# Depthwise convolution accumulated in two PSUM banks, four PSUM banks left for projections, and another order of projections, pooling, layer norm and modulation

## The chip, the cores and the metric

The kernel runs on one core of a Trainium2 chip. Time is the device time of one execution, in microseconds (us). The engines of the core are PE (TensorE: matrix products), DVE (VectorE), ACT (ScalarE), POOL (GpSimd) and SP (SyncE, which here only issues transfers). Matrix products write to PSUM, a memory of eight banks of 128 x 512 float32 each; DVE and ACT read and write PSUM too. Everything else lies in SBUF.

## The reference

One decoder layer over 2048 tokens of width 1024, in float32. A conditioning vector gives shift, scale and gate for both halves. Four mixers of 256 channels share one input projection:

```
def reference(x, c, w_ada, b_ada, norm1_g, ...):
    mod = (silu(c) @ w_ada + b_ada)
    sh1, sc1, g1, sh2, sc2, g2 = split(mod, 6)
    h = rms_norm(x, norm1_g) * (1.0 + sc1) + sh1
    qa, ka, va, ub, uc, ud = split(h @ w_in, IN_SPLITS)
    ya = diff_attention(qa, ka, va, ...)             # 4 heads, causal
    yb = conformer_conv(ub, ...)
    yc = short_gated_conv(uc, short_conv_w)          # bg, cg, xc = uc;  bg * conv3(cg * xc)
    yd = multiscale_pool(ud, pool_w, pool_scale)     # causal means over 2, 4, 8, 16 tokens
    x = x + g1 * (concat([ya, yb, yc, yd]) @ w_out)
    h = rms_norm(x, norm2_g) * (1.0 + sc2) + sh2
    x = x + g2 * (square(relu(h @ w_ff1)) @ w_ff2)
    return x

def conformer_conv(u, dw_w, dw_b, ln_g, ln_b):
    val, gate = split(u, 2)
    h = causal_dwconv(val * sigmoid(gate), dw_w) + dw_b   # 31 taps, each channel by itself
    return silu(layer_norm(h, ln_g, ln_b))
```

## The kernel before

The work stands in three stages one after another: the input projections with everything that belongs to the mixers of convolution, pooling and short convolution; the attention; then output projection and MLP. Each engine has its own program, written out in the order in which it runs; semaphores join them. The change touches the first stage and the first units of the attention.

**The first stage** runs twice, for h = 0 and h = 1, with 1024 tokens each, in eight tiles of 128 tokens (`HT`) and in two blocks of 512 (`NB`). First comes the tile loop. For each tile DVE takes the statistics of x (`mean_square`, L1194 to L1197) and ACT the root (`rms_root`, L827); DVE scales x (`normalise`, L1204); PE transposes it (L1677); ACT applies gain and shift (`modulate`, L836) and rounds to a high part (`h_head`, L842), and DVE takes the rest as a low part (`h_tail`, L1210). Every product of float32 is three matmuls of such parts (`mm3`, L1667 to L1669). PE then projects q, k and v of the tile; ACT and DVE normalise q and k (L869, L873, L1274 to L1284).

Behind the tile loop come projections by columns, called gate, val, ud, cg, pool, xc and bg. Each, pool excepted, is one item of weights: loaded by SP, split by ACT (L820) and DVE (`w_in_tail`, L1215), and multiplied in four pieces, two channel groups cc by two blocks b, with 24 matmuls of 128x512 each. Each piece goes to a PSUM bank, `bank(o)`, the o-th output's bank of a ring: `RING` banks from bank 2 on. PE may begin a piece when the piece `RING` places before it has been read (`free`). ACT reads gate (sigmoid, L912), ud, cg and pool out of PSUM; DVE reads val (multiplied with the gate into `conf`, L1427), xc (L1354) and bg (L1370).

**The convolution** has 31 taps by two channel groups by two blocks, 124 instructions for each h, on DVE. The first of a block (L1301) is x times weight plus bias, and each further one (L1304) adds source times weight to `acc`; all of them work in SBUF. The instructions come from a generator, and `pump(taps, n)` puts the next n of them at a place in DVE's program. A block can begin when its val is there, so the taps of h = 0 run on into h = 1, and those of h = 1 into the attention.

**Layer norm** LN(h, b) of a block is a chain over four engines: PE sums the channels with a matrix of ones (L1747); DVE subtracts the mean (L1320, L1321); ACT squares (L879); PE sums again (L1747, second time); ACT takes the root (L883); DVE the reciprocal and two products (L1327 to L1329); ACT applies gain, bias and a sigmoid (L890, L894); POOL multiplies (L748). `LN_AT` places PE's sums in front of gate, val and bg of h = 1, those of the last block in the attention at unit `LN_STEP`.

**Modulation** of the second half is a product with `w_ada`, taken on the side: SP loads a slice (L521, L522), ACT scales it (L928, two instructions), POOL adds it up (L757, two instructions), and after eight slices k = 0 to 7 PE sums over partitions (`modulation`, L1736) and DVE reads the sum. **Pooling**: POOL adds shifted copies of ud (`windows`, L736 to L741), DVE makes the differences (`pooled`, L1343), PE multiplies (L1798).

In the attention ACT splits q and k of a token tile, POOL forms the low part (`split_tail`, L788), PE transposes (L1831), ACT stacks (L1033), PE forms scores (L1864), DVE reads them (L1484).

## Time and profile before

| | us |
|---|---|
| median of 3 runs | 2618.75 (2618.7 to 2618.93) |
| profiled execution | 2617.26 |
| its span in the trace | 2615.5 |

The profiled execution had a mean granted clock of 0.958 of full speed. The span falls into these stretches, read as start to end in us from the span's start:

| stretch | what runs | length |
|---|---|---|
| 0 to 38 | loads, first modulation sums | 38.0 |
| 38 to 140.5 | tile loop h = 0 | 102.5 |
| 140.5 to 305.7 | gate to bg, h = 0 | 165.2 |
| 305.7 to 394.8 | tile loop h = 1 | 89.1 |
| 394.8 to 566.5 | gate to bg, h = 1 | 171.7 |
| 566.5 to 636.7 | first units of the attention, last taps | 70.2 |
| 636.7 to 2615.5 | rest of the attention, output projection, MLP | 1978.8 |

"Busy" is the time in which an engine executes; PE's busy time beside its stretch tells how much of the stretch PE stands still. A row of the timeline gives start, duration and, in brackets, how long the engine had been idle before it and what released it.

### The profile page before, as it was taken

The numbers are of one execution on the slowest core, as the hardware profiler recorded it, in microseconds if no ns is written. First come the engines' busy times: TensorE is split into PE (matmuls) and PEld (weight loads), VectorE is DVE, ScalarE is ACT, GpSimd is POOL, SyncE is SP. The second block draws the span as 40 slices with busy tenths as digits, with TensorE's granted clock in tenths as the row PEclk, the third lists the DMA queues.
The fourth block names the chain that finished last, engine by engine and source line by source line (L and its number), as shares of the span: only waits on it lengthen the run. The fifth ranks groups of instructions, "written<-read, shape, count | busy, mean of one in ns | idle before, by whom it ended". The sixth has DMA issues, their size and how long they took to land.

```text
span 2615.5 us, 30850 instructions
## 1 busy us (share of the span) xinstructions
PE 2426.9 (93%) x11970; PEld 2031.7 (78%) x11970; DVE 1602.3 (61%) x2301; ACT 871.9 (33%) x1365; POOL 218.5 (8%) x145
## 2 busy tenths in 40 slices
PE   6997898886889888999999999999989999999999
PEld 3985796665878876778888888887868888888887
DVE  3648894998889865655555555555654555555554
ACT  3532253226978853421212121212422121212120
POOL 0233043411221100000000000000000000000000
PEclk9998998987999988999999999999999999999999
DMA  6442234110000014111111111115221111111111
GB/s 229 140 134 73 89 129 145 57 65 25 17 9 25 9 34 144 57 65 49 48 48 48 48 48 48 48 48 185 73 65 49 49 48 48 48 48 48 48 48 64
DMA packets 106998, 176.62 MB, mean 68 GB/s; under 512 B 5000, under 2 KB 76956, under 8 KB 105884
## 3 DMA queue, kind: packets, MB, share of 16 engines
q1 hardware_dynamic: 106908, 175.40, 20.3%
q8 instruction: 59, 0.97, 0.2%
q14 instruction: 31, 0.25, 0.0%
HBM read 152.32 MB, written 23.07 MB: 67 GB/s over the span
## 4 chain that ended last, share of the span: by engine, by line
PE 66%; DVE 16%; issue 7%; DMA 4%; ACT 4%; POOL 2%; SPq 1%; POOLq 0%; ACTq 0%; DVEq 0%
PE ps L1667 18%; PE ps L1668 18%; PE ps L1669 18%; DVE sb_acc L1304 6%; PE ps L1917 2%; PE ps L1919 2%; PE ps L1918 2%; DVE sb_scores L1484 2%; DVE sb_w_lo L1215 2%; PE ps L1831 1%; POOL sb_gate_row L757 1%; PE ps L1846 1%; ACT sb_w_hi L820 1%; PE ps L1864 1%; DMA sb_x_in<-in_x 1%
## 5 line engine op out<-in xcount | busy, mean ns | idle before, releaser
L1667 PE MATMUL ps<-sb_h_hi,sb_w_hi 128*128 128x512 f32 x1408 | 559.1, 397 | 13.1 <-DVE sb_w_lo L1215 11.2
L1668 PE MATMUL ps<-sb_h_lo,sb_w_hi 128*128 128x512 f32 x1408 | 551.5, 392 | 0.0
L1669 PE MATMUL ps<-sb_h_hi,sb_w_lo 128*128 128x512 f32 x1408 | 550.8, 391 | 0.0
L1617 DVE TENSOR_TENSOR sb_x_new<-sb_x_new,ps 128x512 f32<-128x512 f32 x512 | 344.5, 686 | 213.5 <-PE ps L1669 211.3
L1667 PE MATMUL ps<-sb_w_hi,sb_u_hi 128*128 128x512 f32 x1024 | 399.7, 390 | 9.5 <-DVE sb_x_new L1617 9.5
L1668 PE MATMUL ps<-sb_w_lo,sb_u_hi 128*128 128x512 f32 x1024 | 398.9, 390 | 0.0
L1669 PE MATMUL ps<-sb_w_hi,sb_u_lo 128*128 128x512 f32 x1024 | 398.9, 390 | 0.0
L1142 ACT ACTIVATE sb_relu_t<-ps 128x512 f32<-128x512 f32 x128 | 76.1, 594 | 929.0 <-PE ps L1669 868.6
L1667 PEld LDWEIGHTS ps<-sb_h_hi,sb_w_hi 128*128 128x128 f32 x1408 | 266.9, 190 | 74.0 <-DVE sb_w_lo L1215 12.3
L1668 PEld LDWEIGHTS ps<-sb_h_lo,sb_w_hi 128*128 128x128 f32 x1408 | 266.6, 189 | 58.9 <-issue 4.0
L1669 PEld LDWEIGHTS ps<-sb_h_hi,sb_w_lo 128*128 128x128 f32 x1408 | 266.5, 189 | 56.2
L1602 DVE TENSOR_TENSOR sb_relu_t<-sb_relu_t 128x512 f32<-128x512 f32 x128 | 88.7, 693 | 358.1 <-ACT sb_relu_t L1142 358.1
L1215 DVE TENSOR_TENSOR sb_w_lo<-sb_w_raw,sb_w_hi 128x2048 fp32r<-128x2048 f32 x88 | 204.5, 2324 | 106.4 <-ACT sb_w_hi L820 106.4
L1667 PEld LDWEIGHTS ps<-sb_w_hi,sb_u_hi 128*128 128x128 f32 x1024 | 192.6, 188 | 51.8 <-DVE sb_x_new L1617 12.0
L1669 PEld LDWEIGHTS ps<-sb_w_hi,sb_u_lo 128*128 128x128 f32 x1024 | 192.5, 188 | 40.1
L1668 PEld LDWEIGHTS ps<-sb_w_lo,sb_u_hi 128*128 128x128 f32 x1024 | 192.7, 188 | 39.8
L820 ACT ACTIVATE sb_w_hi<-sb_w_raw 128x2048 fp32r<-128x2048 f32 x88 | 168.2, 1911 | 154.4 <-DVE sb_w_raw L1223 68.3
L1304 DVE SCALAR_TENSOR_TENSOR sb_acc<-sb_conf,sb_col,sb_acc 128x512 f32<-128x512 f32 x240 | 208.3, 932 | 0.0
L1484 DVE TENSOR_SCALAR_CACHE_REDUCE sb_scores<-ps 128x1024 f32<-128x1024 f32 (+7 forms) x160 | 138.4, 893 | 47.2 <-PE ps L1867 32.0
L1846 PE MATMUL ps<-sb_v_sb,sb_a_t 128*128 128x64 f32 x1088 | 149.8, 281 | 0.0
L1846 PEld LDWEIGHTS ps<-sb_v_sb,sb_a_t 128*128 128x128 f32 x1088 | 146.4, 207 | 0.5 <-issue 0.5
L1864 PE MATMUL ps<-sb_k_stack,sb_q_stack 128*128 128x512 f32 (+3 forms) x320 | 119.8, 440 | 26.6 <-DVE sb_scores L1484 16.2
(195 smaller groups left out, 3138.8 us busy)
## 6 DMA issues: line engine op xcount, KB each, us to landing
sb_w_raw<-in_w_ff SPq DMA_DIRECT2D x64, 1024.0 KB, 5.2
sb_w_raw<-in_w_in SPq DMA_DIRECT2D x18, 1024.0 KB, 6.0
sb_ada<-in_w_ada SPq DMA_DIRECT2D x32, 512.0 KB, 4.7
sb_ada_first<-in_w_ada SPq DMA_DIRECT2D x8, 1024.0 KB, 7.7
sb_x_in<-in_x SPq DMA_DIRECT2D x16, 512.0 KB, 5.9
sb_x_new<-in_x SPq DMA_DIRECT2D x16, 512.0 KB, 4.6
out<-sb_x_new SPq DMA_DIRECT2D x16, 512.0 KB, 4.9
sb_mix_in<-mix_scratch SPq DMA_DIRECT2D x14, 512.0 KB, 4.3
```

The source lines that it names most:

```text
L820: A(w_hi[s][:, :], raw[:, :], ACT.Copy).then_inc(whi_ready, 1)
L1142: A(relu_t[f][:, :], psum[:, 2 + f % 2, :], ACT.Relu).then_inc(relu_ready, 1)
L1215: V.tensor_tensor(out=w_lo[s][:, :], in0=raw[:, :], in1=f32(w_hi[s][:, :]), op=ALU.subtract).then_inc(wlo_ready, 1)
L1304: ins = V.scalar_tensor_tensor(out=dst, in0=src, scalar=w, in1=dst, op0=ALU.mult, op1=ALU.add)
L1484: V.tensor_scalar(prob(u, m, c0, n), sc_pair(r)[:, 0:n], -SCALE, None, ALU.mult, ALU.min, accum_out=part_min[:, s, m, c0 // WIDE:c0 // WID ...
L1602: V.tensor_tensor(out=relu_t[f][:, :], in0=relu_t[f][:, :], in1=relu_t[f][:, :], op=ALU.mult).then_inc(sq_ready, 1)
L1617: V.tensor_tensor(out=y, in0=y, in1=psum[:, 4 + o % 4, :], op=ALU.add).then_inc(ff2_read, 1)
L1667: M(dst, ah, bh, start=(n == 0), stop=False)
L1668: M(dst, ah, bl, start=False, stop=False)
L1669: ins = M(dst, al, bh, start=False, stop=(n == last))
L1846: ins = M(psum[:, 6 + i % 2, hd * VD:(hd + 1) * VD], a_t[gn % 3][:, k * P:(k + 1) * P], v_sb[:, k0 + k, hd * VD:(hd + 1) * VD], start=(k0 ...
L1864: ins = M(dst[:, 0:w], q_stack[i % 2][:, 2 * hd + m, :], k_stack[:, 2 * hd + m, c0 + b0:c0 + b0 + w], start=True, stop=not diag, skip_grou ...
```

## The change

The convolution writes to PSUM banks 6 and 7 (`conv_bank`), one for each channel group, and `RING` falls from 6 to 4. When a block's 62 taps are done, a new instruction of ACT, `move_conv`, copies both banks to `acc` in SBUF; it raises `conv_moved`, on which wait DVE's first tap of the next block, PE's layer-norm sum and the first product of attention weights with v.

PE's order becomes gate, val, ud, cg, modulation part 0, xc, modulation part 1, pool, bg (before: ud, modulation part 0, cg with part 1 in its middle, pool, xc, bg). PE's layer-norm sums move: LN(0, 0) into the tile loop of h = 1 at tiles 2 and 4, LN(0, 1) in front of val (first sum) and ud (second), LN(1, 0) in front of either block of bg, LN(1, 1) two units earlier. The other engines' parts of it move along. In the tile loop ACT takes the root of a tile before it modulates the tile ahead of it, and DVE takes statistics and scales before `h_tail`; in h = 1 all of this runs one tile further ahead, so tiles 8 and 9 are transposed and modulated within bg of h = 0. The taps are spread anew, with fewer by the end of h = 0 and h = 1, as shown below. POOL runs ln_out of LN(0, 1) between the two blocks' windows, and ln_out of LN(1, 0) behind the attention's first split. `pool_in` and `norm_acc` move to other places in SBUF.

```
     for h in range(2):
         for t in range(0, HT, 2):
+            if h and t in LN_ROWS:
+                out.append(("ln",) + LN_ROWS[t])
             out += [("qk", h, t, 0), ("qk", h, t + 1, 0), ("v", h, t, 0)]
-        for kind in ("gate", "val", "ud", "cg", "pool", "xc", "bg"):
+        for kind in ("gate", "val", "ud", "cg", "xc", "pool", "bg"):
...
-LN_AT = {"gate": (0, 0), "val": (0, 1), "bg": (1, 0)}
+LN_ROWS = {2: (0, 0, 0), 4: (0, 0, 1)}
+LN_COLS = {("val", 0): (0, 1, 0), ("ud", 0): (0, 1, 1), ("bg", 0): (1, 0, 0), ("bg", 1): (1, 0, 1)}
...
-RING = 6
-LN_STEP = 7
+RING = 4
+LN_STEP = 5
...
+        def conv_bank(cc):
+            return psum[:, 6 + cc, :]
...
+            def move_conv(h, b):
+                act.wait_ge(conv_ready, NB * h + b + 1)
+                if h:
+                    act.wait_ge(ln_st[b], 16)
+                A(acc[:, :, b * BLK:(b + 1) * BLK], psum[:, 6:8, :], ACT.Copy).then_inc(conv_moved, 1)
...
-                    if t + 1 < HT:
-                        modulate(n + 1, h_tmp, gain1, shift1)
-                        h_head(n + 1, h_tmp)
-                    if n + 2 < NT:
-                        rms_root(n + 2)
+                    if n + 2 + h < NT:
+                        rms_root(n + 2 + h)
+                    if t + 1 + h < HT:
+                        modulate(n + 1 + h, h_tmp, gain1, shift1)
+                        h_head(n + 1 + h, h_tmp)
...
-                            src, dst = conf[:, cc, b * BLK + j:b * BLK + j + BLK], acc[:, cc, b * BLK:(b + 1) * BLK]
+                            src, dst = conf[:, cc, b * BLK + j:b * BLK + j + BLK], conv_bank(cc)
                             if j == 0:
-                                if h and cc == 0:
-                                    dve.wait_ge(ln_st[b], 16)
+                                if cc == 0 and h + b:
+                                    dve.wait_ge(conv_moved, NB * h + b)
...
-                    pe.wait_ge(conv_ready, h * NB + b + 1)
+                    pe.wait_ge(conv_moved, h * NB + b + 1)
...
                 for i, kind in enumerate(("gate", "val", "ud", "cg")):
-                    project_cols(kind, h, w0 + 3 + i, (lambda: modulation(h, 1)) if kind == "cg" else (lambda: None))
-                    if kind == "ud":
-                        modulation(h, 0)
+                    project_cols(kind, h, w0 + 3 + i)
+                modulation(h, 0)
+                project_cols("xc", h, w0 + 7)
+                modulation(h, 1)
...
+                    pe.wait_ge(conv_moved, 2 * NB)
```

The order is shown where it is spoken of. ACT in the tile loop of h = 0, for the tile t = 1; `sb_h_tmp` is what `modulate` writes, `sb_stat` what `rms_root` writes. Before:

```order
L836 ACTIVATE sb_h_tmp<-ps,sb_shift_62,sb_gain_61 128x128 [waits h_ready,xt_ready]
L836 ACTIVATE sb_h_tmp<-ps,sb_shift_62,sb_gain_61 128x128 x7
L842 ACTIVATE sb_h_hi<-sb_h_tmp 128x8x128 [waits hmod_ready]
L827 ACTIVATE sb_stat<-sb_stat,sb_small 128x1 [waits ms_ready]
L869 ACTIVATE sb_qk_sq<-ps 128x512 [waits proj_ready]
```

And after:

```order
L834 ACTIVATE sb_stat<-sb_stat,sb_small 128x1 [waits ms_ready]
L843 ACTIVATE sb_h_tmp<-ps,sb_shift_62,sb_gain_61 128x128 [waits h_ready,xt_ready]
L843 ACTIVATE sb_h_tmp<-ps,sb_shift_62,sb_gain_61 128x128 x7
L849 ACTIVATE sb_h_hi<-sb_h_tmp 128x8x128 [waits hmod_ready]
L876 ACTIVATE sb_qk_sq<-ps 128x512 [waits proj_ready]
```

The root of tile 3, which waits for DVE's statistics, has moved in front of the modulation of tile 2.

DVE behind the tile loop of h = 1, from the last q and k to the first taps of h = 1. `sb_w_lo_78`, `_79` and `_77` are the low parts of gate's, val's and ud's weights. Before:

```order
L1215 TENSOR_TENSOR sb_w_lo_78<-sb_w_raw,sb_w_hi_74 128x2048 [waits whi_ready]
L1304 SCALAR_TENSOR_TENSOR sb_acc<-sb_conf,sb_col_55,sb_acc 128x512 [waits dve_chain] x5
L1311 COPY sb_conf<-sb_conf 128x2x30 [waits conv_ready]
L1320 TENSOR_TENSOR sb_acc<-sb_acc,ps 128x512 [waits proj_ready,dve_chain]
L1321 TENSOR_TENSOR sb_acc<-sb_acc,ps 128x512
L1215 TENSOR_TENSOR sb_w_lo_79<-sb_w_raw,sb_w_hi_75 128x2048 [waits whi_ready]
L1327 RECIPROCAL sb_ln_rs_97<-sb_ln_rs_97 128x512 [waits lnsd_ready]
L1328 TENSOR_TENSOR sb_acc<-sb_acc,sb_ln_rs_97 128x512 [waits dve_chain]
L1329 TENSOR_TENSOR sb_acc<-sb_acc,sb_ln_rs_97 128x512
L1215 TENSOR_TENSOR sb_w_lo_77<-sb_w_raw,sb_w_hi_73 128x2048 [waits whi_ready]
```

And after:

```order
L1233 TENSOR_TENSOR sb_w_lo_78<-sb_w_raw,sb_w_hi_74 128x2048 [waits whi_ready]
L1322 SCALAR_TENSOR_TENSOR ps<-sb_conf,sb_col_55,ps 128x512 [waits dve_chain] x21
L1331 COPY sb_conf<-sb_conf 128x2x30 [waits conv_ready]
L1233 TENSOR_TENSOR sb_w_lo_79<-sb_w_raw,sb_w_hi_75 128x2048 [waits whi_ready,dve_chain]
L1233 TENSOR_TENSOR sb_w_lo_77<-sb_w_raw,sb_w_hi_73 128x2048 [waits whi_ready]
L1340 TENSOR_TENSOR sb_acc<-sb_acc,ps 128x512 [waits proj_ready]
```

Twenty-one taps in a row now stand in front of val's low part, where five stood, and the wait for the layer norm's root is gone from between the two low parts.

ACT in the same place, from the split of val's weights on; L928 and L942 are slices of the modulation, L912 and L925 are gate read out of PSUM. Before:

```order
L820 ACTIVATE sb_w_hi_75<-sb_w_raw 128x2048 [waits proj_ready,w_ld]
L928 ACTIVATE sb_ada<-sb_ada,sb_silu_c 128x1024 [waits ada_ld]
L928 ACTIVATE sb_ada<-sb_ada,sb_silu_c 128x1024
L912 ACT_TABLE_LOAD [waits proj_ready]
L912 ACTIVATE sb_gated<-ps 128x512 [waits prod_ready]
```

And after, two pieces of gate later:

```order
L925 ACTIVATE sb_gated<-ps 128x512 [waits proj_ready] x2
L942 ACTIVATE sb_ada<-sb_ada,sb_silu_c 128x1024 [waits ada_ld]
L942 ACTIVATE sb_ada<-sb_ada,sb_silu_c 128x1024
L925 ACTIVATE sb_gated<-ps 128x512 [waits proj_ready] x2
L886 ACTIVATE sb_acc<-ps 128x2x512 [waits conv_ready]
```

The copy out of the convolution's banks (L886) stands behind all four pieces of gate and a slice of the modulation that waits for its load.

DVE at the start of the attention; L1484 and L1519 read scores. Before, the last 34 taps stand as three, six times four and ten less; after, as three, six, six and this:

```order
L1535 SCALAR_TENSOR_TENSOR sb_scores_116<-sb_scores_116,sb_ratio 128x128 [waits dve_chain]
L1322 SCALAR_TENSOR_TENSOR ps<-sb_conf,sb_col_55,ps 128x512 [waits dve_chain] x29
L1519 TENSOR_SCALAR sb_scores_117,sb_part_min<-ps 128x128 [waits sc_mm] x2
```

The rest, 29 taps, now stands in one block in front of the scores of unit 3.

## Rows read from the trace of the kernel before

**Rows 1.** The page, part 4: the chain that ended last, by line.
```profile
PE ps L1667 18%; PE ps L1668 18%; PE ps L1669 18%; DVE sb_acc L1304 6%; PE ps L1917 2%; PE ps L1919 2%; PE ps L1918 2%; DVE sb_scores L1484 2%; DVE sb_w_lo L1215 2%; PE ps L1831 1%; POOL sb_gate_row L757 1%; PE ps L1846 1%; ACT sb_w_hi L820 1%; PE ps L1864 1%; DMA sb_x_in<-in_x 1%
```

**Rows 2.** Windows: stretch, length; PE, PEld, DVE, ACT, POOL busy; clock; DMA share, GB/s.
```profile
38.00:140.50 102.50, 84.22 (x647) 81.38 (x645) 61.22 (x90) 55.00 (x110) 20.19 (x19) 0.92 0.40 139
140.50:305.70 165.20, 145.60 (x608) 114.99 (x608) 120.77 (x148) 36.36 (x43) 44.16 (x24) 0.94 0.28 89
305.70:394.80 89.10, 81.49 (x629) 80.16 (x629) 74.68 (x102) 50.71 (x100) 30.06 (x19) 0.92 0.41 138
394.80:566.50 171.70, 153.43 (x614) 117.65 (x612) 130.81 (x152) 49.75 (x56) 52.14 (x29) 0.93 0.25 82
566.50:636.70 70.20, 33.80 (x160) 27.47 (x160) 56.84 (x128) 36.38 (x86) 16.70 (x13) 0.62 0.17 56
...
1000.00:2615.50 1615.50, 1588.28 (x7023) 1311.77 (x7022) 858.30 (x1059) 359.08 (x499) 0.00 (x0) 0.99 0.18 59
```

**Rows 3.** PE's waits, 0 to 700 us: total us, times, longest.
```profile
PE ps L1798 <- DVE sb_pool_in L1343: 17.1, 4, 6.7
PE ps L1747 <- ACT sb_ln_sq L879: 10.7, 2, 10.1
...
PE ps L1747 <- DVE sb_acc L1304: 9.7, 1, 9.7
...
PE ps L1736 <- POOL sb_gate_row L757: 6.8, 1, 6.8
```

**Rows 4.** Lines: all further taps, 38 to 640 us; total busy, mean ns.
```profile
L1304 DVE SCALAR_TENSOR_TENSOR sb_acc<-sb_conf,sb_col,sb_acc 128x512 f32<-128x512 f32 x240 | 208.3, 932 | 0.0
```

**Rows 5.** Timeline, DVE: taps beside POOL's work and without it.
```profile
585.02 4.82 DVE L1304 SCALAR_TENSOR_TENSOR sb_acc<-sb_conf,sb_col,sb_acc 128x512 f32<-128x512 f32 x4
...
603.32 6.71 DVE L1304 SCALAR_TENSOR_TENSOR sb_acc<-sb_conf,sb_col,sb_acc 128x512 f32<-128x512 f32 x10
```

**Rows 6.** Timeline, DVE: two products from PSUM, and two within SBUF.
```profile
413.88 0.69 DVE L1320 TENSOR_TENSOR sb_acc<-sb_acc,ps 128x512 f32<-128x512 f32 x1
414.49 0.68 DVE L1321 TENSOR_TENSOR sb_acc<-sb_acc,ps 128x512 f32<-128x512 f32 x1
...
437.91 0.69 DVE L1328 TENSOR_TENSOR sb_acc<-sb_acc,sb_ln_rs 128x512 f32<-128x512 f32 x1
438.52 0.68 DVE L1329 TENSOR_TENSOR sb_acc<-sb_acc,sb_ln_rs 128x512 f32<-128x512 f32 x1
```

**Rows 7.** Timeline, ACT and DVE: one tile's modulation, its parts, next statistics.
```profile
100.81 2.91 ACT L836 ACTIVATE sb_h_tmp<-ps,sb_shift,sb_gain 128x128 f32<-128x128 f32 x8 [0.36 <-PE ps L1677]
103.75 1.06 ACT L842 ACTIVATE sb_h_hi<-sb_h_tmp 128x1024 fp32r<-128x1024 f32 x1
...
104.84 1.83 DVE L1210 TENSOR_TENSOR sb_h_lo<-sb_h_tmp,sb_h_hi 128x1024 fp32r<-128x1024 f32 x1 [1.59 <-ACT sb_h_hi L842]
...
113.33 0.69 DVE L1194 BATCH_NORM_STATS2 sb_bn<-sb_x_in 128x6 f32<-128x512 f32 x1 [3.85 <-DMA sb_x_in<-in_x]
```

**Rows 8.** Timeline, PE and ACT: gate's first matmuls; gate read out, h = 0.
```profile
142.03 0.39 PE L1667 MATMUL ps<-sb_h_hi,sb_w_hi 128*128 128x512 f32 x1
142.26 0.39 PE L1668 MATMUL ps<-sb_h_lo,sb_w_hi 128*128 128x512 f32 x1
...
168.28 1.09 ACT L912 ACTIVATE sb_gated<-ps 128x512 f32<-128x512 f32 x2
```

**Rows 9.** Timeline, PE: four matmuls after a long wait, and four without.
```profile
212.95 3.78 PE L1736 MATMUL ps<-sb_gate_row,sb_ones_mean 128*128 128x512 f32 x4 [6.83 <-POOL sb_gate_row L757]
...
393.47 1.88 PE L1747 MATMUL ps<-sb_acc,sb_ones_mean 128*128 128x512 f32 x4
```

**Rows 10.** Timeline, DVE and ACT, gate of h = 1: low parts, late modulation slice.
```profile
408.02 2.29 DVE L1215 TENSOR_TENSOR sb_w_lo<-sb_w_raw,sb_w_hi 128x2048 fp32r<-128x2048 f32 x1 [13.13 <-ACT sb_w_hi L820]
...
430.29 2.19 ACT L928 ACTIVATE sb_ada<-sb_ada,sb_silu_c 128x1024 f32<-128x1024 f32 x2 [7.75 <-DMA sb_ada<-in_w_ada]
```

**Rows 11.** Timeline, PE: the last layer norm's sum.
```profile
610.17 2.04 PE L1747 MATMUL ps<-sb_acc,sb_ones_mean 128*128 128x512 f32 x2 [9.66 <-DVE sb_acc L1304]
```

More of the change, by code:

```diff
@@ L538, in store_v, with store_mixer @@
                              qkv_out[s][:, :].rearrange("p (t d) -> p t d", t=2)).then_inc(qkv_st[s], 16)
-            def store_mixer(h, chunk, ready):
-                for b in range(NB):
+            def store_mixer(h, chunk, ready, blocks=range(NB)):
+                for b in blocks:
                     for cc in range(GC):
@@ L924, in scale_ada @@
                     act.wait_ge(mod2_ready, 1)
-                    act.wait_ge(halo_saved, NB * GC)
+                    for q in range(2):
+                        act.wait_ge(stage_st[q], 16 * NB * GC)
                 for n, acc_k in enumerate(mod_sums(h)):
@@ L959, in _ @@
                         scale_ada(h, t // 2)
+                    if h and t == 2:
+                        ln_square(0, 0)
+                    if h and t == 4:
+                        ln_root(0, 0)
                 qk_square(h * HT + HT - 1)
@@ L1407, in _ @@
                         w_in_tail(w0 + 2)
-                    pump(taps, 4)
+                    if h and t == 2:
+                        ln_sub(0, 0)
+                    if h and t == 5:
+                        ln_scale(0, 0)
+                    else:
+                        pump(taps, 4)
                 w_in_tail(w0 + 3)
@@ L1450, in _ @@
                         w_in_tail(NI)
-                    pump(taps, 7)
+                    if (cc, b) != blocks[-1]:
+                        pump(taps, 4 if (cc, b) == (0, 0) and h == 0 else 6)
+                read_gate(h)
                 dve.wait_ge(prod_ready, NB * GC * (h + 1))
@@ L1768, in _ @@
                     n = h * HT + t
-                    if t + 1 < HT:
-                        transposes(n + 1, x_in[(n + 1) % 2])
+                    if t + 1 + h < HT:
+                        transposes(n + 1 + h, x_in[(n + 1 + h) % 2])
+                    if h and t in LN_ROWS:
+                        layer_norm(*LN_ROWS[t])
                     o = OUT_NO["qk", h, t, 0]
```

161 lines of the change are left out of this document (86 added, 75 removed).

## Prediction

> **What bounds the kernel now.** I read the windows first, since an average hides what bounds each stage [rows 2]. From 1000 us to the end PE is busy 1588 of 1615 us at a clock of 0.99; nothing that the change touches lies there. The stages it touches are shorter: in the two tile loops PE stands still for 18.3 and 7.6 us, between gate and bg for 19.6 (h = 0) and 18.3 (h = 1), and at the attention's start for 36.4 of 70.2 us, at a clock of 0.62. Then I read what ended PE's waits up to 700 us [rows 3]: pooled input from DVE 17.1 us in four waits, the square of a layer norm 10.1 in one, the last taps of the convolution 9.7, POOL's modulation sum 6.8. So PE sets the pace, and at a few places DVE's order makes it wait. The chain agrees: three matmul lines have 18% each, the taps 6% [rows 1]. The reader is to see that DVE is no bound as a whole (131 us busy in 172), but is one wherever its queue puts taps ahead of something that PE needs.
>
> What a wait costs beyond itself is in [rows 9]: four matmuls behind a wait of 6.8 us took 3.78 us, four behind none 1.88. I take 1.6 to 3.4 us for the slow clock behind each wait of over 3 us.
>
> **Taps in PSUM.** 248 taps move. In SBUF the 240 further ones between 38 and 640 us took 208.3 us [rows 4]. Ten alone took 6.71 us; with 0.69 for the last, as for a product of that size [rows 6], that is 6.02 / 9 = 0.67 each. Four took 4.82 beside POOL's work [rows 5], where 0.69 + 3 x 0.67 = 2.7 would do. Against 240 x 0.67 = 161 us, some 47 us are lost beside POOL. No row shows a tap that writes to PSUM. From below the nearest row is a product that reads PSUM, and its pair within SBUF: the second of either pair begins 0.61 us after the first [rows 6], so the side of the source costs nothing. I take 0.67 as before. The lower end is 0.61, the spacing of these products; the upper is 0.73, as far above as that is below. Some 130 taps lie on paths that PE waits for (the 21, 20, 41 and 45 or so named below), so the ends are -8 and +8 us. The 47 us of contention should shrink, as a tap now has one input in SBUF; that I count only where DVE is what PE waits for.
>
> The Trainium skill, "VectorE: DVE Perf Modes", in the section on the errata of trn2, has 120 cycles of fixed cost for a source in PSUM against 58 in SBUF, which would be 0.065 us a tap and about 8 us on the path as an estimate; [rows 6] speak against it. The page "SBUF — State Buffer", section "Who interferes with whom", says that a VectorE operation with two inputs in SBUF contends with GpSimd's reads, and one with a single such input doesn't; by that rule the loss in [rows 5] goes.
>
> **Tile loop, h = 0.** ACT now takes the root of tile n+2 before it modulates tile n+1. That root needs x(n+2) to have landed and DVE's statistics. Before, modulation waited only for PE's transposes (0.36 us in [rows 7]). A round of the new chain is statistics 1.8 (two of 0.69 and two short ones), root 0.3, modulation 2.9, high part 1.1, low part 1.2 to 1.8 [rows 7], and by my estimate 1.3 for crossings between engines and 0.6 for the scale: 9.2 to 9.8 us. PE needs about as much for a tile: it is busy 81.5 us for the eight of h = 1, with a few us of layer norm among them [rows 2], so 9.5. There is little slack, and two events fall in: the first root comes late at tile 1 (2 us), and x of tile 7 lands late, since its load stands behind a modulation slice; DVE already waited 3.85 us for such a load [rows 7]. I take +7 us at the start of gate, between 6 and 9.
>
> **Gate to bg, h = 0.** With four banks val's first piece needs gate's first to be read. PE issues 96 matmuls for gate, 0.227 us apart [rows 8]: 21.9 us. ACT read gate 27.8 us after gate began (168.28 against 140.5) since the weights' load and a slice of the modulation stand in front of it. So val waits 5.4 to 6.3 us, plus 1.6 for the clock; with six banks it didn't. Gains: xc fills the time behind the modulation's sum (6.8 and 1.9 of clock [rows 9]) and two of the four waits for pooled input, 9.6 of the 17.1 [rows 3], shrink to about 6, since pool's third and fourth pieces now need xc's banks read by DVE, behind taps. Sum: +7 at the start, +7.6 for val, -9.5 for the modulation (6.8, 1.9 and 0.8 of clock in what follows), -3.6 for pooling and -1.9 for the clock behind the one of its two waits that goes: -0.4 us at the end of bg. If ACT reads gate earlier, val's term falls toward nothing; if pooling isn't relieved, +5.5 come back.
>
> **Tile loop, h = 1.** Two tiles stand ready at its start, so a longer chain of DVE and ACT (the 9.5 us and four taps of 0.67, 12.2 a tile) is felt only late. PE also does 3.6 us of layer-norm sums here, which before stood behind the loop. I take gate at 395.5 against 394.8.
>
> **Gate to bg, h = 1.** Here lies the change's promise and its largest new wait. Removed: the wait of 10.1 us for the square [rows 3], with 3.4 of clock. Added: PE's sum for LN(0, 1) in front of val waits for `conv_moved`, and ACT's copy stands behind all of gate and a slice of the modulation. That slice came at 430.3 [rows 10], 35.5 us after gate began, since its load is issued behind that of a weight item, which waits for a low part of DVE's; and DVE has now 21 taps (14 us) ahead of the next low part. Against that, the 13.1 us in which DVE stood still before its low part [rows 10] take most of these taps. The copy ends at 35.5, 3 for the later low part, 2.2 for the slice [rows 10], 1.1 for two pieces of gate [rows 8], 1.1 for the copy (as long as another instruction of ACT over 1024 elements [rows 7]) and 1 for crossings: 43.9 us after gate's start, and gate's last piece ends at 21.9. I get a wait of 22 us (20 to 23) with 3.4 of clock. So this place is 25.4 - 13.5 = 11.9 us worse. Behind it PE finds everything done: the waits for pooled input (17.1 - 9.6 = 7.5, and 1.6 of clock) go, and with them some 4 us of smaller ones, from the 18.3 us that PE stands still here. Sum: 11.9 - 13.1 + 0.7 from the loop: bg ends 0.5 us earlier than before.
>
> **Attention's start.** The split stands before POOL's layer norm, so the first score comes some 3.5 us earlier by my estimate (a product of POOL and its wait). But 41 taps are left (124 - 83) instead of 34 (124 - 90), and 29 stand in one block: 29 x 0.67 = 19 us in which no score is read. The last taps ended at 610, 35 us after the first score, and PE waited 9.7 us for them [rows 11]. After, the taps end about as early, but units 3 to 6 run behind them, not beside: 2.5 us later by the sum of both, between -1 and +6.
>
> **Sum against the profiled execution.** 2617.26 - 0.5 + 2.5 = 2619.3, rounded to 2619. That execution lies 1.5 us under the median of the runs shown, which is less than the sum's own error, so I leave it at 2619.
>
> **Rivals.** A, slower: the tap in PSUM at 0.73 us, wherever DVE is late (21 taps before val's low part, 20 before the modulation's sum is read, 41 in the attention, some 45 in the tile loops): 130 x 0.06 = +8, 2627. It decides from about 0.71 us a tap, where 130 x 0.04 = 5 us take the sum out of no change. The trace has no tap in PSUM, so it stays possible; [rows 6] speak against it. B, faster: without the contention DVE is 20 to 25 us ahead by the end of each h, the waits for pooled input are gone in both (another -6 and what remains of the clock's price), the wait before val of h = 1 is 16, not 22, since DVE's backlog is less, and the tap costs 0.61: -6 - 6 - 2 = -14, 2605. For it speaks that the change takes work off DVE just where [rows 3] show PE waiting for it; against it that three of the waits hang on ACT's and SP's order, which gets no faster. C: reading and writing the same bank halves DVE's rate on taps: 248 more half-microseconds, of which about 100 us show, 2720. No row speaks for it. D: the layer norm's sum before val waits in full and nothing is given back later, as DVE is still late at pooling: 2617.3 + 11.9 + 0.7 + 2.5 = 2632. It would show as a wait of over 20 us and one of 6 behind it.
>
> **How the numbers follow.** Within 5.2 us of 2618.75, which is 0.2% and about what a measurement of this kernel can tell from no change, lies 2613.5 to 2624. My sum with errors of 5 us: 0.45, which lies mostly within. B 0.30, A 0.14, D 0.08, C 0.03. The chance of faster is B's and a part of the sum's lower tail, 0.37; same 0.31; slower 0.32. The range leaves out C and the outer tails of B and D: 2602 to 2635. The likeliest case alone is 2612 to 2626. The chances of both signs are near each other because the change trades waits of one size for others, and because of one unmeasured price.
>
> **What would show it.** Right: gate of h = 0 begins at 146 to 150 us; val there waits 5 to 6 us; no wait at the modulation's sum; a wait of about 22 us at 418 for ACT's copy; taps of 0.67 us whether POOL works or not; bg of h = 1 ends at 565; taps end at about 607 to 613. Wrong: tiles of h = 0 that keep 9.5 us in spite of the new order; a tap off 0.67 by over 0.04; a wait before val of h = 1 under 15 us, by which the whole gains up to 10.

## Result and the profile after

| kernel | median us | runs |
|---|---|---|
| before | 2618.56 (2615.26 to 2622.96) | 16 |
| changed | 2627.28 (2620.57 to 2630.44) | 16 |

The ratio is 1.0033, 95% interval 1.0025 to 1.004: the change makes the kernel slower by 8.7 us. The time forecast, 2619, is missed by 8.3 us, inside the range of 2602 to 2635. The profiled execution of the changed kernel took 2629.74 us (span 2628.0), 12.5 more than that of before, where the medians differ by 8.7. Of the 12.5 us, 2.8 lie behind the first units of the attention (from 681.3 us on, before from 671.6), which the change doesn't touch, and 1.8 in the start: the first product of q and k began at 55.3 us, before at 53.6, and over the kernels below, whose starts are alike, at 53.2 to 55.3. So an absolute time of one profile can't be compared with that of another to better than 2 us; below, lengths of stretches are compared wherever it matters.

The windows of the changed kernel, by the same stages as [rows 2] (stretch, length; PE, PEld, DVE, ACT, POOL busy; clock; DMA share, GB/s):

```profile
39.00:150.70 111.70, 88.48 (x648) 84.59 (x646) 63.65 (x91) 55.60 (x110) 20.21 (x19) 0.88 0.37 128
150.70:308.10 157.40, 144.10 (x615) 115.08 (x616) 99.23 (x140) 43.23 (x55) 42.37 (x24) 0.97 0.31 99
308.10:404.20 96.10, 84.03 (x627) 80.81 (x625) 65.98 (x97) 45.93 (x89) 21.58 (x19) 0.91 0.35 118
404.20:576.30 172.10, 146.99 (x609) 115.08 (x610) 118.64 (x159) 48.84 (x56) 52.12 (x32) 0.93 0.25 81
576.30:645.80 69.50, 28.78 (x149) 23.11 (x148) 55.21 (x125) 34.93 (x83) 12.45 (x10) 0.66 0.19 65
```

Both tile loops are longer: 111.7 against 102.5 us, and 96.1 against 89.1. Gate to bg is 8 us shorter in h = 0 and about even in h = 1 (172.1 against 171.7), and so is the attention's start. DVE is busy 21 us less in the second stretch and 12 less in the fourth. What ended PE's waits between 39 and 700 us (total, times, longest), beside [rows 3]:

```profile
PE ps L1782 <- ACT sb_acc L886: 25.1, 1, 25.1
PE ps L1902 <- ACT sb_k_stack L1046: 20.5, 1, 20.5
PE ps L1712 <- ACT sb_h_tmp L843: 16.8, 3, 9.3
...
PE ps L1702 <- ACT sb_qkv_out L953: 8.8, 2, 5.2
PE ps L1702 <- ACT sb_gated L925: 6.8, 1, 6.8
...
PE ps L1702 <- DVE sb_qkv_out L1302: 5.2, 2, 3.3
```

Gone are the waits for pooled input, for the square and for POOL's sum. New are five: the copy out of the convolution's banks in front of val (25.1), the block of taps in the attention (20.5), ACT's reads of gate and v (6.8 and 8.8), and DVE's read of q and k (5.2). The last three are waits for a bank of the ring. Of the 16.8 us for `sb_h_tmp` (ACT's modulation), 9.3 stand ahead of the first product of q and k, where before waited 9.1 as well; 6.0 stand at the transposes of the next tile but one, where before waited 5.2 for DVE's scaling.

All further taps, 38 to 650 us, beside [rows 4]; then 21 of them in a row, of which POOL worked beside the last seven only; then six with POOL's work beside all of them:

```profile
L1322 DVE SCALAR_TENSOR_TENSOR ps<-sb_conf,sb_col,ps 128x512 f32<-128x512 f32 x240 | 161.5, 748 | 0.0
...
422.64 13.91 DVE L1322 SCALAR_TENSOR_TENSOR ps<-sb_conf,sb_col,ps 128x512 f32<-128x512 f32 x21
...
202.67 4.04 DVE L1322 SCALAR_TENSOR_TENSOR ps<-sb_conf,sb_col,ps 128x512 f32<-128x512 f32 x6
202.21 4.76 POOL L766 TENSOR_TENSOR sb_gate_row<-sb_gate_row,sb_ada 128x1024 f32<-128x1024 f32 x2 [7.59 <-ACT sb_ada L942]
```

So a tap into PSUM costs (13.91 - 0.69) / 20 = 0.66 us, and (4.04 - 0.69) / 5 = 0.67 beside POOL. All 240 take 161.5 us, against 208.3 before.

One thing that the part on the change says of its order is wrong: `sb_w_lo_78`, `_79` and `_77` there are the low parts of val, ud and cg, and `sb_w_hi_75` is ud's. The 21 taps stand behind val's low part and in front of ud's. PE doesn't wait for that low part, but for the copy that follows the taps.

### The profile page after: what moved, and what is told of

Its sections match the earlier page's. It is cut to its first block, busy times and chain, and to the rows that moved or that the text cites. A ratio compares the mean times of both kernels' runs of the same rounds, so it can differ in the third digit from the quotient of the medians.

```text
span 2628.0 us, 30852 instructions
## 1 busy us (share of the span) xinstructions
PE 2424.3 (92%) x11970; PEld 2031.9 (77%) x11970; DVE 1561.7 (59%) x2300; ACT 872.6 (33%) x1367; POOL 203.8 (8%) x145
## 4 chain that ended last, share of the span: by engine, by line
PE 68%; DVE 13%; issue 6%; ACT 5%; DMA 4%; POOL 2%; SPq 1%; POOLq 0%; ACTq 0%; DVEq 0%
PE ps L1702 19%; PE ps L1703 19%; PE ps L1704 19%; DVE ps L1322 3%; PE ps L1955 2%; PE ps L1957 2%; PE ps L1956 2%; DVE sb_scores L1519 2%; ACT sb_h_tmp L843 2%; DVE sb_w_lo L1233 2%; PE ps L1868 2%; DMA sb_w_raw<-in_w_in 2%; PE ps L1884 1%; POOL sb_gate_row L766 1%; ACT sb_w_hi L827 1%
## 5 line engine op out<-in xcount | busy, mean ns | idle before, releaser
L1702 PEld LDWEIGHTS ps<-sb_h_hi,sb_w_hi 128*128 128x128 f32 x1408 | 266.0, 189 | 77.2 <-DVE sb_w_lo L1233 10.5
L1519 DVE TENSOR_SCALAR_CACHE_REDUCE sb_scores<-ps 128x1024 f32<-128x1024 f32 (+7 forms) x160 | 138.4, 892 | 47.0 <-PE ps L1905 31.5
L1322 DVE SCALAR_TENSOR_TENSOR ps<-sb_conf,sb_col,ps 128x512 f32<-128x512 f32 x240 | 161.5, 748 | 0.0
L1902 PE MATMUL ps<-sb_k_stack,sb_q_stack 128*128 128x512 f32 (+3 forms) x320 | 119.4, 439 | 37.8 <-ACT sb_k_stack L1046 20.5
```

Of the source, the lines that this page charges most:

```text
L1322: ins = V.scalar_tensor_tensor(out=dst, in0=src, scalar=w, in1=dst, op0=ALU.mult, op1=ALU.add)
L1519: V.tensor_scalar(prob(u, m, c0, n), sc_pair(r)[:, 0:n], -SCALE, None, ALU.mult, ALU.min, accum_out=part_min[:, s, m, c0 // WIDE:c0 // WID ...
L1702: M(dst, ah, bh, start=(n == 0), stop=False)
L1902: ins = M(dst[:, 0:w], q_stack[i % 2][:, 2 * hd + m, :], k_stack[:, 2 * hd + m, c0 + b0:c0 + b0 + w], start=True, stop=not diag, skip_grou ...
```

## Experiments

Each kernel is the changed one with the edit named, except where it says otherwise. Each ratio is to before as measured beside it: 2618.2 us for x1 to x4, 2617.4 for x5 to x9, 2620.2 for z1 and z2, 2616.8 for z3. What the text calls less or more is a difference of medians. The changed kernel's ratio is 1.0033 (1.0025 to 1.004); where the intervals of two ratios overlap, as with x2 and x9, the difference isn't resolved.

| kernel | median us | ratio to before (95%) |
|---|---|---|
| x1_copy_early | 2618.40 | 1.0 (0.9989 to 1.0011) |
| x2_v_first | 2624.39 | 1.0019 (1.0007 to 1.003) |
| x3_root_late | 2611.69 | 0.9971 (0.996 to 0.9982) |
| x4_before_ring4 | 2632.99 | 1.0057 (1.0044 to 1.0071) |
| x5_sbuf_taps | 2645.70 | 1.0107 (1.0092 to 1.0121) |
| x6_copy_root | 2604.33 | 0.9949 (0.9933 to 0.9964) |
| x7_taps_earlier | 2622.15 | 1.0011 (1.0 to 1.0022) |
| x9_gate_first | 2627.88 | 1.0035 (1.0022 to 1.0048) |
| z1_no_copy_wait | 2603.47 | 0.9938 (0.9925 to 0.9951) |
| z2_and_taps | 2600.75 | 0.993 (0.9917 to 0.9943) |
| z3_second_half | 2598.29 | 0.9919 (0.9905 to 0.9934) |

### The root ahead of the modulation (x3_root_late)

```
                 for t in range(HT):
                     n = h * HT + t
-                    if n + 2 + h < NT:
-                        rms_root(n + 2 + h)
                     if t + 1 + h < HT:
                         modulate(n + 1 + h, h_tmp, gain1, shift1)
                         h_head(n + 1 + h, h_tmp)
+                    if n + 2 + h < NT:
+                        rms_root(n + 2 + h)
```

On DVE `h_tail` stands between the statistics and the scaling again.

> The changed kernel with the old order in both tile loops: ACT modulates and rounds a tile before it takes the root of the tile ahead, and DVE takes the low part between statistics and scaling. Theory 1, from the prediction (the root ahead of the modulation lengthens the round): gate of h = 0 begins 4 to 7 us earlier than 150.8, gate of h = 1 2 to 5 earlier, and the time is 2619 to 2623. Theory 2 (the ring of four alone makes the loops late): gate of h = 0 stays within 2 us of 150.8, with the waits for the read of q and k still there, and the time within 2 us of 2627.

Measured: 2611.69, 15.6 us less than the changed kernel, a larger gain than either theory gave, and not where the first put it. Gate of h = 0 began at 148.9 us, against 150.75, but this kernel also started 1.7 us earlier: from the first product of q and k to gate it took 95.3 us, the changed kernel 95.4. Nothing was gained there. The wait of 6.0 us for ACT's modulation became one of 5.1 for DVE's scaling, and DVE's read of q and k still cost two bank waits (2.4 and 3.0 us): at h = 0 theory 2 holds. The gain is in the tile loop of h = 1, from its first product of q and k to gate: 82.5 us, against 96.1. The rounds of ACT show it. In the tile loop of h = 1, ACT in the changed kernel:

```profile
326.92 2.88 ACT L843 ACTIVATE sb_h_tmp<-ps,sb_shift,sb_gain 128x128 f32<-128x128 f32 x8
...
338.45 0.29 ACT L834 ACTIVATE sb_stat<-sb_stat,sb_small 128x1 f32<-128x1 f32 x1 [3.28 <-DVE sb_stat L1215]
338.65 2.88 ACT L843 ACTIVATE sb_h_tmp<-ps,sb_shift,sb_gain 128x128 f32<-128x128 f32 x8
...
351.38 0.29 ACT L834 ACTIVATE sb_stat<-sb_stat,sb_small 128x1 f32<-128x1 f32 x1 [3.27 <-DVE sb_stat L1215]
351.58 2.88 ACT L843 ACTIVATE sb_h_tmp<-ps,sb_shift,sb_gain 128x128 f32<-128x128 f32 x8
...
364.99 0.30 ACT L834 ACTIVATE sb_stat<-sb_stat,sb_small 128x1 f32<-128x1 f32 x1 [5.15 <-DVE sb_stat L1215]
365.19 2.88 ACT L843 ACTIVATE sb_h_tmp<-ps,sb_shift,sb_gain 128x128 f32<-128x128 f32 x8
```

ACT stands idle 3.3 to 5.2 us a round for the statistics (the bracket), and DVE takes these behind four taps of the round before; a round is 11.7, 12.9 and 13.6 us, where PE needs 9.5. The prediction's 12.2 us for a round was right, and its "felt only late" was wrong. With the root late, in x3_root_late, the same stretch has a PE that stands still for 3.2 us and a clock of 0.98 (third row of its windows, columns as above):

```profile
307.10:389.60 82.50, 79.28 (x626) 76.35 (x625) 65.00 (x96) 45.99 (x89) 21.63 (x19) 0.98 0.41 138
```

### The ring of four banks (x4_before_ring4, x2_v_first, x9_gate_first)

x4_before_ring4 is the kernel before with one line:

```
-RING = 6
+RING = 4
```

> The kernel before with RING = 4 and nothing else: taps stay in SBUF, the order is the old one, banks 6 and 7 lie idle in the projections. Theory 1 (each piece's bank must be read four pieces later, and readers are late): val of h = 0 waits 5 to 7 us for ACT's read of gate, val or ud of h = 1 waits as well, and the tile loops get waits of 1 to 4 us: 2632 to 2642 against 2618.6. Theory 2 (readers keep up, the ring is seldom full): 2618 to 2624.

Measured: 2632.99, 14.8 us over before; theory 1, in its range. Its waits on PE, 0 to 700 us, with one row that [rows 3] doesn't have:

```profile
PE ps L1667 <- DVE sb_qkv_out L1284: 12.7, 4, 4.9
...
PE ps L1798 <- DVE sb_pool_in L1343: 11.9, 2, 6.7
```

And at val of h = 0:

```profile
177.68 0.77 PE L1667 MATMUL ps<-sb_h_hi,sb_w_hi 128*128 128x512 f32 x1 [6.95 <-ACT sb_gated L912]
```

Gate of h = 0 began at 148.7 us in the old order with four banks, 8.1 later than before, and 7.1 when the later start is taken off. In the changed kernel the same delay is 8.5 (95.4 against 87.0 us from the first product of q and k), and 8.3 with the root late. So some 7 us of it are the ring's, through pieces of q and k whose bank is read late; the root's order adds 0.2 at most, and the last 1.2 us have no cause that these runs show. In the tile loop of h = 1 the ring alone, in the old order, cost 10.5 us (99.5 against 89.1).

x2_v_first moves ACT's read of v to the head of its round:

```
                     n = h * HT + t
+                    if t >= 2 and t % 2 == 0:
+                        copy_v(h, t - 2)
                     if n + 2 + h < NT:
                         rms_root(n + 2 + h)
```

> The changed kernel with ACT's read of v (two tiles' v out of PSUM) moved to the head of a round of the tile loop, before root and modulation of the tiles ahead. In the changed kernel PE waits 5.2 and 3.7 us in the tile loop of h = 1 for this read, since v's bank is the fourth in the ring and must be free. Theory 1 (ring of four couples PE to ACT's round): both waits fall to under 2 us, gate of h = 1 begins some 6 us earlier than 404.2, and the time is 2621 against 2627; h = 0 keeps its waits of 1.9 and 3.3 us, which are for DVE's read of q and k. Theory 2 (DVE and ACT are late in h = 1 whatever the ring): the waits turn up as waits for the low part of h, and gate begins at 403 or later.

Measured: 2624.39. The waits for v's read were gone, as theory 1 had it, and the loop of h = 1 took 90.9 us, 5.1 less. But the edit works in both loops: that of h = 0 took 2.9 us more and the stretch from gate to q and k of h = 1 1.8 more, so that gate of h = 1 began at 402.5 and not at 398. PE had four other waits in the loop of h = 1, 8.1 us in all, at the start of tiles:

```profile
PE ps L1702 <- issue: 8.1, 4, 3.2
...
347.74 0.69 DVE L1302 TENSOR_TENSOR sb_qkv_out<-ps,sb_small 128x512 f32<-128x512 f32 x1
348.53 0.36 PE L1702 MATMUL ps<-sb_w_hi,sb_h_hi 128*128 128x256 f32 x1 [2.01 <-issue]
```

The profile names no event for them, but each of the four ends 0.1 us after DVE's read of a q and k piece, as here, and PE's program waits there for a bank of the ring: they are bank waits again. The four tiles begin at 336.8, 348.5, 361.5 and 375.2 us, 11.7, 12.9 and 13.7 apart, as long as ACT's rounds. So from the third tile on PE goes at ACT's and DVE's pace, whichever read it waits for. That is neither theory whole: reading v early is worth 5.1 us of this loop, the order of the root 13.5 (x3_root_late, where v's read cost PE 1.9 and 0.8 us with the ring still at four). Both work through the ring of four. What the early root would cost with six banks was not run.

x9_gate_first has ACT read gate's first two pieces ahead of the split of ud's weights and of the modulation slice:

```
-                w_in_head(w0 + 5)
-                scale_ada(h, 4)
...
-                each_block("gate", h, to_gated(ACT.Sigmoid), lambda: scale_ada(h, 5))
+
+                def middle():
+                    w_in_head(w0 + 5)
+                    scale_ada(h, 4)
+                    scale_ada(h, 5)
+
+                each_block("gate", h, to_gated(ACT.Sigmoid), middle)
```

> The changed kernel with ACT's read of gate's first two pieces ahead of the split of ud's weights and of the modulation slice, for both h; the rest of the order is kept. Theory 1 (ring of four: val's first piece waits for this read and for nothing else): the wait of 6.8 us at val of h = 0 is gone, bg of h = 0 ends some 7 us earlier or the gain shows as a longer wait for pool or x behind it; the time falls by 4 to 8 us to 2619 to 2623. At h = 1 nothing changes, since val waits there for the copy. Theory 2 (the time is given back at the tiles 8 to 10, which hang on x's load and DVE): within 2 us of 2627.

Measured: 2627.88, no change, and neither theory's way. Val's first piece no longer waited, but its third did, 6.7 us, for gate's third piece, which ACT now read behind the same split and slice:

```profile
188.14 0.79 PE L1706 MATMUL ps<-sb_h_hi,sb_w_hi 128*128 128x512 f32 x1 [6.72 <-ACT sb_gated L925]
```

With four banks and items of four pieces, each piece of val needs the same piece of gate: the edit moved the wait by two pieces. It says nothing on whether the 6.8 us are worth removing; z1_no_copy_wait does.

### The copy in front of val (x1_copy_early)

In the changed kernel, around gate of h = 1: SP's issues, the taps and the low part behind them on DVE, and ACT.

```profile
422.80 16.81 SPq L503 DMA_DIRECT2D sb_w_raw<-in_w_in  x2
439.66 0.57 SPq L527 DMA_DIRECT2D sb_ada<-in_w_ada  x1
...
436.87 2.29 DVE L1233 TENSOR_TENSOR sb_w_lo<-sb_w_raw,sb_w_hi 128x2048 fp32r<-128x2048 f32 x1
...
447.19 2.19 ACT L942 ACTIVATE sb_ada<-sb_ada,sb_silu_c 128x1024 f32<-128x1024 f32 x2 [10.30 <-DMA sb_ada<-in_w_ada]
449.28 1.06 ACT L925 ACTIVATE sb_gated<-ps 128x512 f32<-128x512 f32 x2
450.24 1.02 ACT L886 ACTIVATE sb_acc<-ps 128x1024 f32<-128x1024 f32 x1
...
451.40 3.75 PE L1782 MATMUL ps<-sb_acc,sb_ones_mean 128*128 128x512 f32 x4 [25.07 <-ACT sb_acc L886]
```

The taps end at 436.55, ud's low part at 439.16; only then can SP issue the next weights, and behind them the modulation's slice (439.66); ACT scales it at 447.19, reads gate, and copies at 450.24. The copy itself could have run 13 us earlier, when the taps had ended. The edit:

```
-                each_block("gate", h, to_gated(ACT.Sigmoid), lambda: scale_ada(h, 5))
-                if h:
-                    move_conv(0, 1)
+                def middle():
+                    if h:
+                        move_conv(0, 1)
+                    scale_ada(h, 5)
+
+                each_block("gate", h, to_gated(ACT.Sigmoid), middle)
```

> The changed kernel with one move on ACT: at gate of h = 1 the copy out of the convolution's banks (move_conv) stands between gate's second and third piece, ahead of the modulation slice whose load comes late, and not behind all of gate. In the changed kernel ACT made this copy at 450.2 us, while the taps it needs had ended at 436.6. Theory 1 (ACT's order makes PE wait): the copy comes at about 438, PE's wait of 25.1 us before val falls to 12, and 13 us less stay to the end, less a few given back at the next waits: 2616 against 2627. Theory 2 (the wait covers work of DVE that is late anyway): the 13 us turn up again as waits behind it (low parts of weights, pooled input), and the time stays within 3 us of 2627.

Measured: 2618.40, 8.9 us less. The wait fell to 12.1 us, and 3.7 came back at val's second piece, for gate. Theory 1, though 2.4 us short of its 2616. In the two profiles only 5.3 us of the gain lie between gate and bg of h = 1; between x3_root_late and x6_copy_root below, which differ by the same edit, it is 7.4 there and 7.4 in the medians. Of the remaining 12 us, the copy began 0.3 us after the last tap (434.5), and ACT was busy until then too.

### Taps in SBUF again (x5_sbuf_taps)

```
-                            src, dst = conf[...], conv_bank(cc)
+                            src, dst = conf[...], acc[:, cc, b * BLK:(b + 1) * BLK]
...
-                A(acc[:, :, b * BLK:(b + 1) * BLK], psum[:, 6:8, :], ACT.Copy).then_inc(conv_moved, 1)
+                A(acc[:, :, b * BLK:(b + 1) * BLK], acc[:, :, b * BLK:(b + 1) * BLK], ACT.Copy).then_inc(conv_moved, 1)
```

A third edit lets the first tap of a block wait for the store of the layer norm's output, which reads `acc`, as before.

> The changed kernel with all taps accumulated in SBUF as before; ACT's move_conv stays where it is, as a copy of the same size in place, so every order, wait and the ring of four banks are kept. It prices the place of the accumulation by itself. In the changed kernel 240 taps take 161.5 us on DVE, before 208.3. Theory 1 (the two SBUF inputs of a tap collide with POOL's work, and some of that is on PE's path): taps take about 205 us again, and the time rises by 5 to 15 us over the changed kernel's 2627, through later pooled input, later low parts of x and a later end of the last block. Theory 2 (where taps stand beside POOL's work, PE isn't waiting for DVE): DVE's time rises the same way, but the total by less than 3 us.

Measured: 2645.70, 18.4 us over the changed kernel, beyond theory 1's 15. DVE's lines, 38 to 650 us, and the same six taps as above beside POOL:

```profile
L1324 DVE SCALAR_TENSOR_TENSOR sb_acc<-sb_conf,sb_col,sb_acc 128x512 f32<-128x512 f32 x240 | 199.8, 900 | 0.0
L1233 DVE TENSOR_TENSOR sb_w_lo<-sb_w_raw,sb_w_hi 128x2048 fp32r<-128x2048 f32 x18 | 49.4, 2742 | 69.2 <-ACT sb_w_hi L827 69.1
...
199.48 8.34 DVE L1324 SCALAR_TENSOR_TENSOR sb_acc<-sb_conf,sb_col,sb_acc 128x512 f32<-128x512 f32 x6
```

The taps take 38.3 us more (199.8 against 161.5) and the low parts 4.1 (49.4 against 45.3), and nearly half of that reaches the end: pooling's waits for xc's read rose from 3.5 to 10.7 us in four, v's from 8.8 to 11.4, and gate of h = 1 began at 416.0, 4.1 of it a wait for its low part. The place of the accumulation is thus worth 18.4 us, in this order. The six taps took 8.34 us with both inputs in SBUF, 4.04 with one: that a tap with one input in SBUF stays free of POOL's work agrees with the rule named in the prediction, of the Trainium skill, "SBUF — State Buffer", "Who interferes with whom". The 0.065 us more for a source in PSUM, which the prediction worked out from the Trainium skill, "VectorE: DVE Perf Modes", section on the errata of trn2, doesn't show: a tap that reads and writes PSUM took 0.66 us, as one in SBUF without POOL (0.67 by [rows 5]).

### Both helpful edits, and six taps (x6_copy_root, x7_taps_earlier)

> Both edits that helped most, together: the copy out of the convolution's banks between gate's second and third piece (alone 8.9 us less than the changed kernel), and the root behind the modulation in both tile loops (alone 15.6 us less). Theory 1 (two separate places on PE's path, the gains add): 2627.3 - 8.9 - 15.6 = 2602.8, between 2600 and 2606, with the wait before val of h = 1 near 14 us. Theory 2 (part of the second gain came from the same slack as the first): 2608 to 2612.

Measured: 2604.33, 23.0 us less than the changed kernel, where the single gains sum to 24.5. They lie at separate places and add, within what these medians can tell.

```
                 read_gate(h)
+                if h:
+                    pump(taps, 6)
                 dve.wait_ge(prod_ready, NB * GC * (h + 1))
```

> The changed kernel with six more taps of h = 1 placed where DVE stood idle for 4 us, behind its read of the modulation's sum and ahead of the layer norm's mean; so the block in front of unit 3 of the attention has 23 taps and not 29. Theory 1 (the block is what PE waits 20.5 us for): that wait falls by 4 us, to 16.5, and the time by 3 to 4 us to 2623 or 2624. Theory 2 (the wait is ACT's order or transfers at the attention's start): the wait keeps 19 us or more, the time stays within 1.5 us of 2627.

Measured: 2622.15, 5.1 less, with the wait at unit 4's scores down from 20.5 to 15.8 us:

```profile
611.40 0.58 PE L1904 MATMUL ps<-sb_k_stack,sb_q_stack 128*128 128x256 f32 x1 [15.84 <-ACT sb_k_stack L1046]
```

The wait fell by 4.6, six taps' 4.0 and a little. Gate to bg of h = 1 was 2.7 us longer in this profile, but 2.0 of that are a longer wait for the copy before val (27.0), ahead of the taps moved; in x3_root_late and x9_gate_first, whose order there is the changed kernel's too, that wait was 26.8. The block of taps is what PE waits for in the attention.

### No wait in front of val (z1_no_copy_wait, z2_and_taps, z3_second_half)

All three have the root late. In z1, DVE runs the 21 taps ahead of val's low part, and ACT's order at gate is: gate's first two pieces, val's split, the copy, a slice, gate's other two, ud's split, the next slice.

```
-                w_in_tail(w0 + 4)
                 pump(taps, 9 * TAPS)
+                w_in_tail(w0 + 4)
```

> The changed kernel with the root behind the modulation in both tile loops, and with what gate's end waits for put in order: DVE runs the 21 last taps of h = 0 while the weights of val are still on their way (in the changed kernel it stood idle for 14.3 us there, and had the taps behind them); ACT reads gate's first two pieces before it splits val's weights, copies the convolution's banks right behind that split, and reads gate's other two before ud's weights. Theory 1 (the 25 us wait is made of order alone, and the ring's wait at val of h = 0 is its reader's order): no wait of over 3 us before val in either h; against the kernel with the copy moved alone and the root behind (2604.3, waits of 11.7 and 2.7 us there and 5.0 at h = 0) that is 15 to 20 us less with the clock's share, 2584 to 2590. Theory 2 (DVE's work is only shifted and PE meets it later, at ud, at the modulation's sum or at pool): 2594 or more, with a new wait of over 6 us behind val of h = 1.

Measured: 2603.47. No wait of over 3 us before val in either h, but the time is 0.9 us under x6_copy_root's, where 15 to 20 were expected; by the ratios, 0.9938 and 0.9949, the difference is not resolved. The time is theory 2's; its sign, one wait of over 6 us behind val of h = 1, is not there, but several smaller ones are. The 19 us of waits taken away came back almost whole. At h = 0 bg ended at 307.1 us, against 300.8 in x6. POOL shows why. Its last modulation slice and the first window, in x6_copy_root and then in z1_no_copy_wait:

```profile
212.36 6.83 POOL L766 TENSOR_TENSOR sb_gate_row<-sb_gate_row,sb_ada 128x1024 f32<-128x1024 f32 x2 [7.43 <-ACT sb_ada L942]
219.27 1.06 POOL L745 TENSOR_TENSOR sb_win_a<-sb_ud 128x527 f32<-128x527 f32 x1
```

```profile
215.82 6.76 POOL L766 TENSOR_TENSOR sb_gate_row<-sb_gate_row,sb_ada 128x1024 f32<-128x1024 f32 x2 [7.89 <-ACT sb_ada L942]
222.66 1.06 POOL L745 TENSOR_TENSOR sb_win_a<-sb_ud 128x527 f32<-128x527 f32 x1
...
PE ps L1840 <- DVE sb_prod L1378: 15.2, 5, 4.7
```

(The last row is from z1's waits on PE, 140 to 560 us.) The slices come one after another through one buffer, and each one that ACT takes later makes the last one later: windows, pooled input, the 20 taps behind them and DVE's read of xc all follow, and PE waits 9.1 us there at h = 0, where it waited 2.5 in x6_copy_root; the other 6.1 of the 15.2 are at h = 1. At h = 1 gate to bg took 163.4 us, against 166.6, though 14.4 us of waits were gone in front of val: new there are 4.6 and 2.0 us for the layer norm at ud, and xc's read grew from 2.2 to 6.1.

> The same kernel with six more taps of h = 1 ahead of the layer norm's mean, so that 23 and not 29 stand before unit 3 of the attention. Where this was done alone it took 4.6 us off PE's wait of 20.5 and 5.1 us off the time, with 1 to 2 us of that given back before the attention. Theory 1 (DVE still stands idle at that place): 3 to 5 us less than its neighbour in this call. Theory 2 (with the waits before val gone, DVE is behind PE at this place): within 1.5 us of its neighbour, and PE's wait for pool, bg or the scores grows by as much as the block's wait falls.

Measured: 2600.75, 2.7 less than z1; the two intervals overlap. PE's wait for the block fell from 19.8 to 15.8 us. The end of bg came 1.6 later, but that arose ahead of gate of h = 1, where the two kernels are the same; gate to bg took 163.1 us, against 163.4. So it is no sign of theory 2.

z3 leaves ACT's order at gate of h = 0 as in the changed kernel.

> The kernel with six taps moved and the waits before val in order, but for h = 0 ACT keeps the changed kernel's order at gate. In its neighbour without this, val of h = 0 no longer waited, but POOL's last modulation slice ended at 222.6 against 219.2 us, and with it the pooling windows, and bg of h = 0 ended at 307.1 against 300.8. Theory 1 (at h = 0 the end is set by the chain of modulation slices, windows and pooled input, and val's wait is cover): bg of h = 0 ends at 301 to 302 again, with the wait of 5 us back at val, and the time is 4 to 6 us under 2600.8: 2595 to 2597. Theory 2 (the later end of h = 0 came from elsewhere, or is given back in h = 1): 2600 or more.

Measured: 2598.29, ratio 0.9919, 1.3 us above theory 1's range, and by the intervals not resolved from z2. Bg of h = 0 ended at 302.6 us, against 308.1, with a wait of 7.0 at val back and the wait for xc's read in h = 0 down from 9.1 to 3.1 (9.2 with that of h = 1):

```profile
PE ps L1846 <- DVE sb_prod L1382: 9.2, 3, 3.4
PE ps L1713 <- ACT sb_gated L925: 7.0, 1, 7.0
```

At h = 0 the wait at val is cover: the chain of slices and windows sets the end, by the profiles; the medians alone don't show it. This version is 0.81% faster than the kernel before (0.66 to 0.95) and 29 us faster than the changed one.

## Why the prediction was right or wrong

The two profiled executions by stretch, as change against before in us. The forecast is the prediction's own; the ends are the first product of q and k, gate and the end of bg of each h, and the first product of a late unit (681.3 us, before 671.6).

| stretch | forecast | measured |
|---|---|---|
| start | 0 | +1.8 |
| tile loop h = 0 | +7 | +8.5 |
| gate of h = 0 to q and k of h = 1 | -7.4 | -7.8 |
| tile loop h = 1 | +1.1 | +7.0 |
| gate to bg, h = 1 | -1.2 | +0.5 |
| attention's start | +2.5 | -0.2 |
| all behind | 0 | +2.8 |
| sum | +2.0 | +12.5 |

In the stretches that the change touches, +2.0 was forecast and +8.0 measured, which is near the 8.7 of the medians. The time fell inside the range; the step that failed is the tile loop of h = 1, 5.9 us too cheap, and the other errors (+1.5, -0.4, +1.7, -2.7) cancel by luck.

- **Taps.** Taken at 0.67 us whether POOL works or not; measured 0.66. Right, with both ends of the range too wide.
- **Tile loop, h = 0.** Forecast +7 us at gate from the root's place; measured +8.5. The size was about right and the step wrong. With four banks alone the old order already has gate 7.1 later (x4_before_ring4), and taking the root back gave 0.2 (x3_root_late). The prediction looked for the ring's price only from gate on; pieces of q, k and v use the same ring. That the number came out near is luck.
- **Gate to bg, h = 0.** The wait at val of 5.4 to 6.3 us came as 6.8, the modulation's went, pooling's of about 6 came as 3.5. The stretch from gate to the end of bg became 153.7 us, where -0.4 - 7 on 161.1 makes 153.7. The mechanism was right; that the number is exact is partly luck, as the terms were off by 1 and 2.5 us.
- **Tile loop, h = 1.** This step failed: gate at 395.5 forecast, 404.2 measured. Of the 8.7 us, 1.8 are the start and 1.1 what h = 0 added; 5.9 are this loop, 96.1 us where some 90.2 were forecast. Its rounds were priced at 12.2 us and measured at 11.7 to 13.6, but two tiles of lead were taken to make them felt only late. They were felt from the third tile on. A lead of two tiles, 19 us, would by itself cover six rounds that lose 3. PE's waits say why it didn't: they are for banks that ACT or DVE empties late in its round (v in the changed kernel, q and k in x2_v_first), which the lead doesn't help. That is read from the waits; an early root with six banks would settle it and was not run. Taking the root back makes the loop 82.5 us long, and is worth 15.6 us of the total.
- **Gate to bg, h = 1.** A wait of 22 us for the copy, 20 to 23: measured 25.1; the waits behind it gone: right. Together 170.5 us forecast (395.5 to 566.0), 172.2 measured, against 171.7 before. One long wait took the place of three shorter ones, as forecast. The 3.4 us for the clock behind it came from no row: the layer-norm sum and val's 96 matmuls behind the wait took 2.3 us more than the next such sum and 96 matmuls behind no wait. x1_copy_early shows that half of the wait was order alone.
- **Attention.** Taps end at 607 to 613: 612.4. Forecast +2.5 us; the first product of the late unit moved by 9.7 us where bg's end had moved by 9.9: -0.2. Too dear.
- **Rival A** gave 2627 and the time is 2627, but by a dearer tap, which didn't come; its number is a coincidence. **Rival B**'s mechanism is real: without the relief from POOL's work the change would have cost 27 us and not 9 (x5_sbuf_taps). But the new waits for the ring and the copy outweighed it. **Rival C**'s halved rate didn't come. **Rival D** foresaw the wait before val, but with late pooling behind it, which wasn't there. Slower, which came, had a chance of 0.32.

## What to carry to other kernels

A ring of output banks is shared by everything that runs through it: when it gets shorter, check each producer against the reader of the piece that many places back, loops far from the change included. A lead of some tiles hides a slower round only if PE needs nothing else from the engines that are late; look for the bank or buffer that they empty in each round. Before a long wait is taken away, follow the other chains to the same end: here 19 us of waits in front of val came back almost whole, in h = 0 through a chain of transfers and sums that goes through one buffer.
